# Four 128x128 products of the token mixer as 64x64 block products in the four quadrants of TensorE

## What is computed

```python
kk = heads(k * k_k)
kk = kk / jnp.maximum(jnp.sqrt(jnp.sum(kk * kk, axis=-1, keepdims=True)), 1e-12)      # "norm"
...
y = wkv7(r_h, heads(decay), k_h, v_h, kk, a_h)                                        # the recurrence
mu = jnp.mean(y, axis=-1, keepdims=True)                                              # "centring"
var = jnp.mean(jnp.square(y - mu), axis=-1, keepdims=True)                            # "variance"
yn = ((y - mu) * lax.rsqrt(var + LN_X_EPS)).reshape(bn, s, D_RWKV)
yn = yn * ln_x_w + ln_x_b
bonus = jnp.sum(r_h * k_h * r_k, axis=-1, keepdims=True) * v_h                        # "bonus"
y_rwkv = (yn + bonus) * (sigmoid(gd) @ gate_up)                                       # "gup"
```

## Time and profile before

| | |
|---|---|
| median of 3 runs | 4411.86 us (4409.42 to 4412.15) |
| the profiled execution | 4404.34 us, its span 4402.5 us |
| PE busy | 4022.2 us, 91% of the span |
| DVE, ACT, POOL busy | 1843.2, 1332.3, 468.1 us |
| mean granted TensorE clock | 0.963 |

### The profile page before, as it was taken

How to read it: one execution, slowest core, us unless ns; L and a number is a source line. 1 busy time by engine, 2 the same in 40 slices (tenths; PEclk the granted TensorE clock), 3 DMA queues, 4 the chain that set the end, 5 groups by cost and what they waited for, 6 DMA issues and landing times.

```text
span 4402.5 us, 93154 instructions
## 1 busy us (share of the span) xinstructions
PE 4022.2 (91%) x36187; PEld 2801.7 (64%) x36187; DVE 1843.2 (42%) x3765; ACT 1332.3 (30%) x2995; POOL 468.1 (11%) x519
## 2 busy tenths in 40 slices
PE   5699999999999999999999999999779999999992
PEld 3477787787787787777777778755444444444440
DVE  3345555555555555555545545532521111111115
ACT  3223333343343343343333333343301111111114
POOL 1001201201201201200200200100000000000003
PEclk8799999999999999999999999999889999999996
DMA  9621221212212212212212212223289999999999
GB/s 328 222 67 50 84 66 57 84 52 71 84 42 81 84 42 81 84 42 81 83 44 78 84 45 70 87 83 133 77 349 411 411 411 411 411 411 411 411 411 374
DMA packets 292930, 760.52 MB, mean 173 GB/s; under 512 B 16466, under 2 KB 107828, under 8 KB 292532
## 3 DMA queue, kind: packets, MB, share of 16 engines
q1 hardware_dynamic: 273876, 687.60, 42.1%
q0 software_dynamic: 11520, 41.95, 2.4%
q10 hardware_dynamic: 7136, 25.23, 1.4%
HBM read 679.19 MB, written 75.52 MB: 171 GB/s over the span
## 4 chain that ended last, share of the span: by engine, by line
PE 85%; issue 5%; DVE 3%; SPq 2%; DMA 2%; ACT 2%; DVEq 0%; POOL 0%; ACTq 0%; POOLq 0%
PE duo L1057 24%; PE bank L1057 10%; PE bank L1417 10%; PE bank L1421 5%; PE bank L1447 5%; PE bank L1287 5%; PE bank L1451 3%; PE duo L1186 2%; PE duo L1184 2%; PE duo L1163 2%; PE duo L1157 1%; PE bank L1120 1%; PE bank L1104 1%; PE duo L1398 1%; PE bank L1106 1%
## 5 line engine op out<-in xcount | busy, mean ns | idle before, releaser
L1057 PE MATMUL duo<-hs,w 128*128 128x256 f32 x5120 | 1141.3, 381 | 28.1 <-ACT at L1483 25.4
L1057 PEld LDWEIGHTS duo<-hs,w 128*128 128x128 f32 x5120 | 969.1, 190 | 220.1 <-issue 33.8
L1057 PE MATMUL bank<-hs,w 128*128 128x256 f32 x2048 | 462.9, 379 | 0.0
L1417 PE MATMUL bank<-W,xT 128*128 128x512 f32 x1024 | 446.4, 594 | 2.2 <-DVE xT L2476 1.5
L1057 PEld LDWEIGHTS bank<-hs,w 128*128 128x128 f32 x2048 | 389.1, 190 | 52.9
L1417 PEld LDWEIGHTS bank<-W,xT 128*128 128x128 f32 x1024 | 192.7, 191 | 233.3 <-issue 233.3
L1483 ACT ACT_TABLE_LOAD x254 | 325.9, 1283 | 11.1 <-issue 6.1
L2482 DVE TENSOR_TENSOR gsig<-bank,gsig 128x512 f32<-128x512 f32 x48 | 33.2, 692 | 675.2 <-ACT gsig L1483 675.2
L819 POOL TENSOR_TENSOR Tm<-Tm,idents 128x512 f32<-128x512 f32 x32 | 40.5, 1267 | 1966.7 <-DVE Tm L2191 1966.7
L1421 PE MATMUL bank<-W,xT 128*64 128x512 f32 x1024 | 228.6, 602 | 18.8 <-issue 18.8
L1287 PE MATMUL bank<-wo,mT 128*128 128x512 f32 x512 | 231.8, 599 | 0.0
(11 more groups left out here) (409 smaller groups left out, 6297.6 us busy)
## 6 DMA issues: line engine op xcount, KB each, us to landing
W<-in_w_expert_in_dram SPq DMA_DIRECT2D x128, 2048.0 KB, 25.4
W<-in_w_expert_out_dram SPq DMA_DIRECT2D x64, 2048.0 KB, 25.4
hs<-h_s SPq DMA_DIRECT2D x224, 512.0 KB, 4.5
w<-in_w_in_dram SPq DMA_DIRECT2D x128, 256.0 KB, 4.2
adaw<-in_w_ada_dram SPq DMA_DIRECT2D x12, 2048.0 KB, 13.3
y_s<-ysb ACTq DMA_DIRECT2D x48, 512.0 KB, 6.7
xt<-in_x_dram SPq DMA_DIRECT2D x16, 512.0 KB, 11.6
WAc<-rank_s SPq DMA_DIRECT2D x32, 256.0 KB, 3.2
```

What stands on the lines that cost most here:

```text
L1057: ins = mm(place(pr, n), w[:, pr, n, k, :], hs[:, n, k, :], start=n < 4 and k == 0, stop=k == KH - 1, skip_group_check=True)
L1417: ins = mm(GU[half][:, :], xT[:, slot, kk_, :], ring_rows(parts[0])[:, k, cols], start=kk_ == 0, stop=kk_ == KT - 1)
```

## The change

`norm` and `centred` become one group of four 64x64 block products, `variance` and `bonus` another. Since the matrices are block-diagonal, each product of 128x128 is two blocks. The blocks of `center` and `rkbd` stay on the diagonal of the array and go to M1. Those of `ones_bd` go crosswise and to M0: head 0 is read from rows 0 to 63 and written to partitions 64 to 127, head 1 the other way, so the readers of M0 swap the halves back: DVE's maximum and ACT's Ln become two instructions of 64 partitions each. `bonus` moves from the end of pair 3 to the middle of pair 2, from M0 to M1, and DVE's `bv` with it, to behind `post`. `gup` moves from M1 to M0.

```diff
+            def blocks(bk, weights, x, crossed):
+                for r in range(2):
+                    o = 1 - r if crossed else r
+                    ins = mm(bk[HALF[o], :], weights[HALF[r], HALF[r]], x[HALF[r], :], start=True, stop=True)
+                return ins
+
+            def norm_and_centred(i):
+                q = prior2(i)
                 pe.wait_ge(S["ksq_ready"], i + 1)
                 pe.wait_ge(S["a_ready"], i + 1)
-                if prior2(i) is not None:
-                    pe.wait_ge(S["yT_summed"], i - 1)
                 if not first(i):
                     pe.wait_ge(S["branch"], i * 3)
-                mm(M0[:, :], ones_bd[:, :], sq[:, :], start=True, stop=True).then_inc(S["norm_done"], 1)
+                if q is not None:
+                    pe.wait_ge(S["yT_summed"], q + 1)
+                    pe.sem_inc(S["pair_go"])
+                    blocks(M1, center, yT, False).then_inc(S["center_done"], 1)
+                blocks(M0, ones_bd, sq, True).then_inc(S["norm_done"], 1)
+
+            def variance_and_bonus(i):
+                q = prior2(i)
+                pe.wait_ge(S["rk_ready"], i + 1)
+                pe.wait_ge(S["rkbd_ready"], i + 1)
+                if q is not None:
+                    pe.wait_ge(S["yc_step"], q * 2 + 2)
+                    pe.sem_inc(S["pair_go"])
+                    blocks(M0, ones_bd, sq, True).then_inc(S["var_done"], 1)
+                blocks(M1, rkbd, rk, False).then_inc(S["bonus_done"], 1)
 
             def gup(i):
                 ...
                 if prior2(i) is None:
-                    pe.wait_ge(S["P_step"], i * 2 + 2)
-                else:
-                    pe.wait_ge(S["yc_step"], i * 2 - 2)
-                mm(M1[:, :], UP[:, 2, :], GDc[:, :], start=True, stop=True).then_inc(S["gup_done"], 1)
-            def bonus(i):
-                ...
+                    pe.wait_ge(S["norm_max"], i + 1)
+                else:
                     pe.wait_ge(S["rs_step"], i * 2 - 3)
-                mm(M0[:, :], rkbd[:, :], rk[:, :], start=True, stop=True).then_inc(S["bonus_done"], 1)
+                mm(M0[:, :], UP[:, 2, :], GDc[:, :], start=True, stop=True).then_inc(S["gup_done"], 1)
@@ head, tail
                 pair(i, 1, range(4))
-                norm(i)
-                if q is not None:
-                    centred(q)
+                norm_and_centred(i)
                 pair(i, 1, range(4, NPROD))
                 ...
                 pair(i, 2, range(2))
-                if q is not None:
-                    variance(q)
+                variance_and_bonus(i)
                 pair(i, 2, range(2, NPROD))
                 pair(i, 3)
-                bonus(i)
                 gup(i)
@@ ACT rstd
-                fn(rs[:, :], bk[:, :], ACT.Ln, scale=1.0 / HD, bias=epsc[:, 1:2]).then_inc(S["rs_step"], 1)
+                    fn(rs[HALF[0], :], M0[HALF[1], :], ACT.Ln, scale=1.0 / HD, bias=epsc[HALF[0], 1:2])
+                    fn(rs[HALF[1], :], M0[HALF[0], :], ACT.Ln, scale=1.0 / HD, bias=epsc[HALF[1], 1:2])\
+                        .then_inc(S["rs_step"], 1)
@@ DVE step
-                V.tensor_scalar(rn[:, :], M0[:, :], 1e-24, None, ALU.max).then_inc(S["norm_max"], 1)
+                V.tensor_scalar(rn[HALF[0], :], M0[HALF[1], :], 1e-24, None, ALU.max)
+                V.tensor_scalar(rn[HALF[1], :], M0[HALF[0], :], 1e-24, None, ALU.max).then_inc(S["norm_max"], 1)
                 ...
                 if q2 is not None:
                     post(q2, p)
                     dve.wait_ge(S["merged_ready"], i - 1)
+                dve.wait_ge(S["bonus_done"], i + 1)
+                dve.wait_ge(S["shifted"], i * 3 + 3)
+                V.tensor_tensor(bv[p][:, :], M1[:, :], vt[:, :], ALU.mult).then_inc(S["branch"], 1)
                 ...
                 V.tensor_tensor(conv[p][:, :], cg[:, :], chs[:, :], ALU.mult).then_inc(S["branch"], 1)
-                dve.wait_ge(S["bonus_done"], i + 1)
-                V.tensor_tensor(bv[p][:, :], M0[:, :], vt[:, :], ALU.mult).then_inc(S["branch"], 1)
                 ...
-                V.tensor_tensor(gg[p][:, :], M1[:, :], gg[p][:, :], ALU.mult).then_inc(S["branch"], 1)
+                V.tensor_tensor(gg[p][:, :], M0[:, :], gg[p][:, :], ALU.mult).then_inc(S["branch"], 1)
```

More of the change, by code:

```diff
@@ L988, in zaaa @@
                 mm(SC[:, :], UP[64:128, 1, :], WAc[64:128, :], start=True, stop=True).then_inc(S["zaaa_done"], 1)
-            def norm(i):
+            def blocks(bk, weights, x, crossed):
[5 more added lines that the diff above has]
+                q = prior2(i)
                 pe.wait_ge(S["ksq_ready"], i + 1)
                 pe.wait_ge(S["a_ready"], i + 1)
-                if prior2(i) is not None:
-                    pe.wait_ge(S["yT_summed"], i - 1)
                 if not first(i):
                     pe.wait_ge(S["branch"], i * 3)
-                mm(M0[:, :], ones_bd[:, :], sq[:, :], start=True, stop=True).then_inc(S["norm_done"], 1)
+                if q is not None:
[12 more added lines that the diff above has]
+                blocks(M1, rkbd, rk, False).then_inc(S["bonus_done"], 1)
             def gup(i):
@@ L1004, in gup @@
                 if prior2(i) is None:
-                    pe.wait_ge(S["P_step"], i * 2 + 2)
-                else:
-                    pe.wait_ge(S["yc_step"], i * 2 - 2)
-                mm(M1[:, :], UP[:, 2, :], GDc[:, :], start=True, stop=True).then_inc(S["gup_done"], 1)
-            def bonus(i):
-                pe.wait_ge(S["rk_ready"], i + 1)
-                pe.wait_ge(S["rkbd_ready"], i + 1)
-                if prior2(i) is None:
                     pe.wait_ge(S["norm_max"], i + 1)
@@ L1246, in head @@
             def head(i):
-                q = prior2(i)
                 zdec(i)
@@ L1585, in centre, with rstd @@
                 fn(sq[:, :], bk[:, :], ACT.Square).then_inc(S["yc_step"], 1)
-            def rstd(q, bk=M0):
+            def rstd(q, bk=None):
                 act.wait_ge(S["var_done"], q + 1)
-                fn(rs[:, :], bk[:, :], ACT.Ln, scale=1.0 / HD, bias=epsc[:, 1:2]).then_inc(S["rs_step"], 1)
+                if bk is None:
+                    fn(rs[HALF[0], :], M0[HALF[1], :], ACT.Ln, scale=1.0 / HD, bias=epsc[HALF[0], 1:2])
+                    fn(rs[HALF[1], :], M0[HALF[0], :], ACT.Ln, scale=1.0 / HD, bias=epsc[HALF[1], 1:2])\
+                        .then_inc(S["rs_step"], 1)
+                else:
+                    fn(rs[:, :], bk[:, :], ACT.Ln, scale=1.0 / HD, bias=epsc[:, 1:2]).then_inc(S["rs_step"], 1)
                 act.wait_ge(S["rs_step"], q * 2 + 1)
```

## The result

The changed kernel takes 4496.98 us (median of 4 runs, 4485.49 to 4503.02), the kernel before in the same comparison 4410.64: a ratio of 1.0188, 95% interval 1.0172 to 1.0205. It is slower by 86 us, and the forecast was 30 us faster.

A forecast was written before the change was run, and what follows sets the result against it. TensorE was taken to set the time (85% of the chain). Steps 2 to 31 save 31.8 us, steps 0 and 1 lose 1.3, net 30.5: from 4411.86 to about 4381 us, range 4366 to 4400.

The forecast's parts named there:

- A fp32 block product of 512 columns in each quadrant, four at once: In each new group, four block products run at once and cost two passes, 0.86 us, instead of four, 1.72 us.
- Switching 0.33 us a group: TensorE's switch into 64x64 blocks and back, with first weights, adds 0.33 us, making a group 1.19 us.
- The sum, 30 us: Over the projections: 1.06 us saved in each of steps 2 to 31, 1.3 lost in steps 0 and 1, net 30.5.
- DVE and ACT hide their added work: Halved maximum and Ln (0.6 us each) and moved `bv` (0.68) stay hidden; rival of lateness: 4400 us, chance 0.08.
- The shared bank: Rival: row halves take turns on M1 or M0, a group takes 2.05 us, time 4437, slower; chance 0.05.
- Code loading moves, up to 15 us: Rival: TensorE's pauses without releaser shift, 4366 to 4396 us; chance of more than 8 us taken 0.14, given 0.07.

The follow-up runs named there:

- after_pad224: The changed kernel with 224 more semaphore increments at the very start of TensorE's stream: 4418.83 us, ratio 1.0018 to the kernel before.
- after_free64: The changed kernel with 64 semaphore increments in TensorE's idle time before the first step: 4494.64 us, ratio 1.0196 to the kernel before.

## Why the prediction was wrong

- *A fp32 block product of 512 columns in each quadrant, four at once:* right. Starts 0.02 us apart, second passes 0.48 later.
- *Switching 0.33 us a group:* right, 1.21 us a group measured against 1.19.
- *The sum, 30 us:* nearly. A step's projections became 0.97 us shorter (54.53 to 53.56 at equal places), where 1.06 was forecast; over the mixer 15 and 25 us in the profiled executions at equal places. The medians show 18 to 20.
- *DVE and ACT hide their added work:* right in the result; the projections keep their saving. How tight it gets was wrong: `bv` was to eat into the 1.15 us ahead of pair 3's sum and leave 0.3. It leaves 0.70 to 0.84 in the steps in which POOL works and 1.15 in the others. In the step shown it ran at 1700.00, ahead of the convolution, and DVE still waits 1.35 us at 1704.67, between the two.
- *The shared bank:* the two halves of one product, from two row halves of the array into one bank, start at 1680.91 together. The rule of the Trainium skill that was weighed, "TensorEngine Tiling (Array Packing)", Gotcha 1, does not bind here, where the halves lie on different partitions: taking turns would have made a group 2.05 us, and it took 1.21.
- *Code loading moves, up to 15 us:* this is the term that failed; the forecast sum had it at nothing, and the rival capped it at 15 us. It was sized by one line's 21.5 us and by how little code was added (0.8%). Measured, with no product changed, the 16 instructions a step cost 104.5 us (4410.64 to 4515.16), and the groups give 18 back: that is the 86. The price is not proportional to the code; it is set by where five block ends fall in each inverse. Over the places run, the pauses range from 48 to 152 us, and the kernel before stood at a fairly good place. The change moved it by 32 records in the even steps and 49 in the odd ones, and as its step is 8 blocks long, both kinds of step got the same bad place.

The account of the profiled executions: span +93.9 us; projections -25.6 (1689.0 to 1663.4 over 31 steps), inverse +114.8 (896.8 to 1011.6), outside the mixer +4.7. Of the inverse's, 74.4 are idle time (101.1 to 175.5): its pauses without a releaser grew by 82.0 (67.1 to 149.1), its waits for ACT and DVE shrank by the rest. The other 40.4 are longer records (795.7 to 836.1), and these go with the clock: in the inverse it stood at its lower level, 1.2 GHz, for 147 us instead of 68. Behind 300 us each such stretch had a pause of this kind in it or in the 3 us before; the one near 260 us had none, in either kernel. Over the 14 kernels of the table, each us more at 1.2 GHz goes with 0.38 us more of records (a straight line through them; correlation 0.96), by which 30 of the 40 are the clock's. That the pauses bring the clock down is argued from their moving together, not shown by a run of its own.

The evidence was in the profile of before: a queue named "instruction" with 303 packets and 4.96 MB, pauses without a releaser that end 255 to 257 records apart, and the rows. The prediction read the second line of the earlier trace rows as inverse and recurrence, but a third of its 45.16 us is the next step's projections. The inverse alone burns 720 + 718 records in 30.16 us, where the projections burn 237 + 234 in 52 (a step has some 945 matmuls, not 1015). An upper bound, worked from that: up to five ends a step, up to 2 us each, 32 steps, 320 us, against 70 in use. With that, a slowdown of this size could have had a chance, where 15 us was taken for the most that code could cost.

The Trainium skill, "Runtime: NRT & Kernel Launch", Instruction fetch mechanics, states that code comes in blocks of 16 KiB or 256 instructions, and that crossing a boundary is mostly hidden. The trace agrees with the size (304 packets for 4.98 MB) and not with the hiding: 151 us of pauses in the changed kernel.

What stays open: why the packet comes so late. Theory 1 says that it is asked for only at the end of the block before, at a cost of 2.4 us less what is queued; the runs show the place and the packet, not that mechanism, and two readings do not fit its number. Six pauses of the changed kernel are longer than the time since their packet began to move, up to 3.6 us against 2.4, so TensorE stood still before it moved. And increments cross the end of a block almost for nothing: in `after_pad224` they start 0.15 us apart; record 199 takes 0.31 us and ends at 31.29, the packet begins to move at 32.02, and none of the increments behind it takes longer than 0.22. So the pause depends on what instructions stand at the end, and the traces do not say why. And no program was built in which TensorE needs no new code in the mixer, so what all the pauses together cost is a sum, not a measured difference.

## What to carry to other kernels

- Products with block-diagonal matrices, several of them ready at once, are worth running as blocks in all four quadrants: two pairs of products became two groups, 0.97 us a step, though each group takes 0.35 us more than its two passes (1.21 against 0.86), which is the switching there and back.
- Where an engine runs many short instructions from a long stream, count its code in blocks of 256 and look for pauses without a releaser at that distance. Any edit that changes the number of instructions moves them, and may win or lose far more than what it was made for: here 18 to 20 us of gain against a swing of 106.
- Compare two versions at equal places: fill the shorter with instructions that do nothing. And once an edit is good, try a few shifts. The changed kernel with 128 increments ahead of it beats both, at 4389 us (0.9956, 0.9942 to 0.9970). And read the whole idle time of the stretch: a pause that has gone can come back as a wait for another engine, as the 17 us for DVE did.

## What the runs showed of the hardware

- A pause at the end of a code block ended 2.2 to 2.9 us after the packet of 16 KB began to move; in the projections, with 0.22 to 0.43 us of work in one pass, no pause was longer than 0.45 us in 13 of the 14 kernels (0.59 in `after_free64`).
- In the first three steps of 14 kernels, 71 of 71 pauses over 0.5 us ended at record 193 to 195 of a block of 256, counted from the start of the program.
- A semaphore increment takes TensorE's sequencer about 0.15 us: from 128 of them at the start to 224 the first product moved from 20.55 to 35.39 us, 14.84 / 96. Sixteen a step cost nothing in the projections (54.58 and 54.56 us).
- The same instructions, shifted by 32 records, changed this kernel's time by 1.5%; shifted by 256, the time was the same to 2 us.
